# A two-layer Hyena / Mamba-2 / mixture-of-experts step: earlier modulation pieces, waits moved across stage seams, and the router in batches

## The reference

```python
sh1, sc1, g1, sh2, sc2, g2 = split(silu(cond) @ ada_w + ada_b, 6)   # once for the context, once for the latents
h = rmsnorm(x, g) * (1 + sc1) + sh1
u = dwconv(h @ in_w + in_b, short_w, short_b)                       # 3072 channels, 3 taps: x0, x1, v
f = sin(freq * (z @ w1 + b1)); f = sin(freq * (f @ w2 + b2))        # filter net, width 64
h_fwd, h_bwd = (f @ w3) * window
v = fft_long_conv(v * x1, h_fwd, h_bwd) + (v * x1) * bias
x = x + g1 * ((v * x0) @ out_w)
h2 = rmsnorm(x, g) * (1 + sc2) + sh2
aff = softmax(h2 @ w_router)                                        # 16 experts
gate, idx = top_k(aff.T, cap)                                       # 128 latent and 16 context rows an expert
x = x + g2 * scatter_add(gate * experts(h2[idx]))
```

## Time and profile before

| | us |
|---|---|
| median of three runs | 3776.02 |
| the profiled execution, its own time | 3775.25 |
| its span | 3773.3 |
| TensorE busy | 3405.7 (90%) |
| VectorE busy | 1868.8 (50%) |
| ScalarE busy | 1297.2 (34%) |
| GpSimd busy | 369.8 (10%) |

### The profile page before, as it was taken

How to read it: one execution, slowest core, us unless ns; L and a number is a source line. 1 busy time by engine, 2 the same in 40 slices (tenths; PEclk the granted TensorE clock), 3 DMA queues, 4 the chain that set the end, 5 groups by cost and what they waited for, 6 DMA issues and landing times. The chain is left out here.

```text
span 3773.3 us, 58905 instructions
## 1 busy us (share of the span) xinstructions
PE 3405.7 (90%) x24069; PEld 2934.9 (78%) x24069; DVE 1868.8 (50%) x3059; ACT 1297.2 (34%) x2067; POOL 369.8 (10%) x361
## 2 busy tenths in 40 slices
PE   4999888979499999998799999779996599999996
PEld 2999764748399999997699999746664499999995
DVE  6233286855533333333544554689996533333333
ACT  4232332224133333333532233266664133333332
POOL 0000000000011111111000000000000011111111
PEclk7999898989699999999799999989997799999998
DMA  6566323054588888885334443397776488888885
GB/s 233 165 207 207 108 83 148 33 195 168 190 289 289 289 289 289 289 288 171 86 106 131 148 142 105 126 341 245 257 255 230 154 290 289 289 289 289 289 289 193
DMA packets 413304, 799.49 MB, mean 212 GB/s; under 512 B 22135, under 2 KB 107836, under 8 KB 411851
## 3 DMA queue, kind: packets, MB, share of 16 engines
q1 hardware_dynamic: 383724, 699.32, 52.8%
q0 software_dynamic: 29232, 98.14, 8.8%
q10 hardware_dynamic: 208, 0.10, 0.0%
HBM read 688.59 MB, written 108.90 MB: 211 GB/s over the span
## 5 line engine op out<-in xcount | busy, mean ns | idle before, releaser
L2192 PEld LDWEIGHTS moe_banks<-moe_xt,mix_ring 128*128 128x128 f32 x8192 | 1012.6, 191 | 5.5 <-issue 3.2
L2192 PE MATMUL moe_banks<-moe_xt,mix_ring 128*128 128x144 f32 x8192 | 1013.9, 287 | 3.1 <-ACT moe_xt L2227 3.1
L62 PE MATMUL ssdin_banks<-h_leading,ssdin_w_split 128*128 128x384 f32 x1920 | 412.0, 344 | 0.0
L2272 DVE TENSOR_TENSOR moe_hid<-moe_banks,moe_sg 128x128 f32<-128x128 f32 x256 | 74.6, 291 | 582.2 <-ACT moe_sg L2250 582.2
L2214 PE MATMUL moe_banks<-moe_down_parts,moe_hid_parts 128*128 128x512 f32 x1536 | 357.5, 392 | 0.0
L62 PEld LDWEIGHTS ssdin_banks<-h_leading,ssdin_w_split 128*128 128x128 f32 x1920 | 337.2, 188 | 14.4 <-issue 13.6
L2214 PEld LDWEIGHTS moe_banks<-moe_down_parts,moe_hid_parts 128*128 128x128 f32 x1536 | 285.9, 188 | 71.3 <-issue 13.2
L2262 DVE TENSOR_TENSOR moe_down_parts<-mix_ring,moe_down_parts 128x2048 fp32r<-128x2048 f32 x128 | 292.2, 2283 | 0.0
L3151 PE MATMUL scan_banks<-scan_w,scan_yc 128*128 128x512 f32 x576 | 254.8, 596 | 0.0
L62 PE MATMUL hyin_banks<-h_leading,hyin_w_split 128*128 128x384 f32 x1152 | 238.0, 338 | 11.5 <-DVE hyin_w_split L751 11.5
L2159 POOL DMA_INDIRECT x_dram<-moe_yc,mix_idx_quarter x128 | 166.3, 1299 | 820.1 <-DVE moe_yc L2283 790.8
(11 more groups left out here) (442 smaller groups left out, 4448.5 us busy)
## 6 DMA issues: line engine op xcount, KB each, us to landing
mix_ring<-in_moe_w_gate SPq DMA_DIRECT2D x64, 2048.0 KB, 8.1
mix_ring<-in_moe_w_up SPq DMA_DIRECT2D x64, 2048.0 KB, 13.1
mix_ring<-in_moe_w_down SPq DMA_DIRECT2D x64, 2048.0 KB, 16.0
early_ring<-in_ada_w SPq DMA_DIRECT2D x96, 512.0 KB, 5.4
scan_cum<-row_dram SPq DMA_DIRECT2D x36, 1024.0 KB, 6.2
ssd_w<-in_ssd_in_w SPq DMA_DIRECT2D x40, 512.0 KB, 4.1
s_dram<-ssdin_work SPq DMA_DIRECT2D x64, 256.0 KB, 2.1
scan_states<-s_dram SPq DMA_DIRECT2D x32, 512.0 KB, 7.7
```

What stands on the lines that cost most here:

```text
L62: ins = pe.matmul(out(piece), w_at(w[a], k), h_k(h[b], k, piece), start=(k == 0 and a == 0 and b == 0), stop=(k == KD - 1 and a == 1))
L2192: ins = pe.matmul(pb[:, 2 * (f % 2) + j, 0:SLOTS], ring[:, 2 * half + j, k, col:col + P], xt[:, k, :], start=(k == 0), stop=(k == KD - 1))
L2272: dve.tensor_tensor(hid[:, f % 2, :], up[:, 0:CAP_LAT], sg[:, f % 2, 0:CAP_LAT], ALU.mult).then_inc(s_hid, 1)
```

## The change

In the opening TensorE multiplies piece 0 ahead of the parameter rows, piece 1 ahead of the filter's first layer, pieces 2 and 3 behind it in the two banks of pieces 0 and 1, and the filter's second layer after all pieces. VectorE's list follows, with the first position add ahead of the gain columns. The second angles and the second sine move into the projection (angles ahead of VectorE's first tile, sine behind ScalarE's second; TensorE waits for the angles before its second tile). `front_h` gets three buffers. The first two weight splits of the projection move into the last rounds of the opening's tile loop. To make that possible, the opening and the projection share one set of banks, and the filter's buffers lie under those of the split rows.

At the seams: the last x0 and u stores of the projection are issued by SyncE and waited for in the convolution, by SyncE before it loads u and by ScalarE before its first filter copy; the g stores are waited for in the output projection, before its first load; the last two x stores of the scan are waited for in the second router, before the loads of those tiles. In the convolution one ScalarE copy (the context row, L1186) moves ahead of `keep_filter(5)`.

VectorE subtracts the trailing part of the same two splits in the same round. `HF` is 3. The class `Router` gets the scheme of `phase_route`: partial logits, a summing matmul, the logits kept, softmax in batches of five and four tiles. In both routers the exponential, the quotients and the transposes of the first batch move into the loop.

```diff
@@ phase_front
-        hf = m.sb("h", [P, 2, KD, P])
+        hf = m.sb("h", [P, HF, KD, P])
-        PIECE_BANK = (3, 4, 5, 6)
+        PIECE_BANK = (3, 4, 3, 4)
@@ tensor
+                pe.wait_ge(s_silu, 2)
+                mod.product(pe, 0, pb[:, PIECE_BANK[0], 0:P])
                 pe.wait_ge(s_stage, 16 * (len(keep["param_rows"]) + 6))
...
-                pe.wait_ge(s_silu, 2)
+                mod.product(pe, 1, pb[:, PIECE_BANK[1], 0:P])
                 filt.products(pe, pb, 0)
-                mod.product(pe, 0, pb[:, PIECE_BANK[0], 0:P])
-                mod.product(pe, 1, pb[:, PIECE_BANK[1], 0:P])
-                filt.products(pe, pb, 1)
-                mod.product(pe, 2, pb[:, PIECE_BANK[2], 0:P])
-                mod.product(pe, 3, pb[:, PIECE_BANK[3], 0:P])
+                for n in range(2, FRONT_PIECES):
+                    pe.wait_ge(s_row, n - 1)
+                    mod.product(pe, n, pb[:, PIECE_BANK[n], 0:P])
                 pe.wait_ge(s_row, FRONT_PIECES)
...
+                filt.products(pe, pb, 1)
@@ phase_front, scalar
+                    if t == TILES:
+                        for q in range(2):
+                            act.wait_ge(keep["s_hy_w"][q], 16)
+                            act.activation(split[:, q, 0, :, :], w[:, q, :, :], ACT.Copy).then_inc(s_wh, 1)
@@ phase_hyena_in
+                sp.wait_ge(s_cv, HY_TILES)
+                store_x0(sp, LAST_BLOCK, keep["s_last_stored"])
+                sp.wait_ge(s_ur, HY_TILES)
+                store_u(sp, LAST_BLOCK, keep["s_last_stored"])
...
+                    if q == 1:
+                        filt.sine(act, 1)
...
+                filt.angles(dve, pb, 1)
@@ phase_long_conv
-                    keep_filter(5)
                     act.wait_ge(s_u, h * 16 + 16)
                     act.activation(win_r[:, 0, :], ut[:, 0, :], ACT.Copy).then_inc(s_zh, 1)
+                    keep_filter(5)
                     keep_filter(6)
...
-                sp.wait_ge(s_gs, 16 * 2 * CT_HALF)
@@ class Router
+    def partial_logits(self, pe, t):
...
+        for k in range(KD):
+            j = k % 4
+            ins = pe.matmul(self.part[self.COLS * j:self.COLS * (j + 1), :], self.wr[:, k, :], self.ht[:, k, :],
+                            start=(k < 4), stop=(k >= 4))
...
     def logits(self, pe, t):
...
-        for k in range(KD):
-            ins = pe.matmul(self.logit, self.ht[:, k, :], self.wr[:, k, :], start=(k == 0), stop=(k == KD - 1))
+        pe.matmul(self.logit, self.parts[:, :], self.adder[:, :], start=True, stop=True).then_inc(self.s_lg, 1)
@@ phase_hyena_out
+                sp.wait_ge(keep["s_g_stored"], 16 * KD)
                 load_g(0)
...
                     if t < TILES:
                         project(t, 0)
-                    if 2 <= t <= TILES + 1:
-                        router.logits(pe, t - 2)
-                    if t >= 3:
-                        router.turn_affinities(pe, t - 3)
+                    if t >= 2:
+                        router.partial_logits(pe, t - 2)
                     if t < TILES:
                         project(t, 1)
+                    if t >= 2 and t <= TILES:
+                        router.logits(pe, t - 2)
                     if 1 <= t <= TILES:
                         router.turn(pe, t - 1)
+                    if t == TILES:
+                        router.turn_affinities(pe, 0)
+                router.logits(pe, TILES - 1)
+                router.turn_affinities(pe, 1)
@@ phase_route
+                    if t >= TILES - 2:
+                        sp.wait_ge(keep["s_scan_x_stored"][t % 2], 16 * (t // 2 + 1))
                     load_x(t)
@@ phase_scan
-                for b in range(2):
-                    sp.wait_ge(s_st[b], 16 * (5 - b))
```

More of the change, by code:

```diff
@@ L174, in phase_front @@
         stage = m.sb("stage", [P, 4, P])
-        filt = Filter(m, io, keep["filt"], keep["prm"])
+        filt = keep["filter_net"]
+        filt.weights(m)
+        HF = 3
+        w, split = keep["hy_w"], keep["hy_split"]
+        s_wh, s_wl = keep["s_hy_lead"], keep["s_hy_rest"]
         d_all = m.sb("d_all", [P, 1, HEADS])
@@ L383, in _ @@
                 dve.wait_ge(s_done, 4)
+                piece(1)
                 filt.angles(dve, pb, 0)
+                piece(2)
+                piece(3)
                 dve.wait_ge(s_d, 16)
@@ L410, in _ @@
                         tile_evict(t - 1)
+                    if t == TILES:
+                        for q in range(2):
+                            dve.wait_ge(s_wh, q + 1)
+                            dve.tensor_tensor(split[:, q, 1, :, :], w[:, q, :, :], split[:, q, 0, :, :].bitcast(F32),
+                                              ALU.subtract).then_inc(s_wl, 1)
 def modulation_columns(dve, keep, layer, c, ks, shift, scale, s_gain):
@@ L569, in phase_hyena_in @@
         w = keep["hy_w"]
-        split = m.sb("w_split", [P, 2, 2, KD, P], F32R)
+        split = keep["hy_split"]
+        filt = keep["filter_net"]
         pad = m.sb("pad", [P, 2, GAPPED + 2])
@@ L838, with __init__ @@
     WIDTH = FOLD // PIECES
-    def __init__(self, m, io, filt, prm):
-        self.io, self.filt = io, filt
+    BANK = (0, 5)
+    def __init__(self, nc, m, io, filt, prm, columns, later):
+        self.io, self.filt, self.col = io, filt, columns
         self.bias, self.freq = [prm[:, 3, F_ROW + n:F_ROW + n + 1] for n in range(2)], prm[:, 3, F_ROW + 2:F_ROW + 3]
-        self.z = m.sb("tap_clock", [HY_EMB, TAPS])
-        self.w1 = m.sb("f_w1", [HY_EMB, HY_HID])
-        self.w2 = m.sb("f_w2", [P, HY_HID])
-        self.col = m.sb("f_columns", [P, 2])
-        self.arg = m.sb("angle", [P, FOLD])
-        self.turns = m.sb("turns", [P, FOLD])
-        self.h1 = self.turns
+        with ExitStack() as until_lead:
+            self.z, arg, turns = [until_lead.enter_context(nc.sbuf_tensor("filter_" + name, shape, F32)) for name, shape in
+                                  (("clock", [HY_EMB, TAPS]), ("angle", [P, FOLD]), ("turns", [P, FOLD]))]
+        self.arg, self.turns = (arg, later[:, 0:FOLD]), (turns, later[:, FOLD:2 * FOLD])
+        self.h1 = turns
         self.s_in = m.sem("filter_in")
@@ L875, in products @@
                     w, src = self.w1[:, :], self.z[:, half * FOLD + cols:half * FOLD + cols + self.WIDTH]
-                ins = pe.matmul(pb[at, n, 0:self.WIDTH], w, src, start=True, stop=True)
+                ins = pe.matmul(pb[at, self.BANK[layer] + n, 0:self.WIDTH], w, src, start=True, stop=True)
         ins.then_inc(self.s_mm, 1)
@@ L1617, in _ @@
                 lead(1)
-                for t in range(TILES + 3):
-                    if 2 <= t <= TILES + 1:
-                        router.exps(act, t - 2)
+                for t in range(TILES + 2):
+                    if t >= 2:
+                        router.keep_parts(act, t - 2)
                     if 1 <= t <= TILES:
@@ L1627, in _ @@
                         lead(t + 2)
+                    if t == TILES - 1:
+                        router.exps(act, 0)
+                router.exps(act, 1)
             @block.gpsimd
@@ L1709, in _ @@
                 position(1)
-                for t in range(TILES + 3):
-                    if 2 <= t <= TILES + 1:
-                        router.top(dve, t - 2)
-                    if t >= 3:
-                        router.keep_affinities(dve, t - 3)
-                    if 2 <= t <= TILES + 1:
-                        router.soft(dve, ch, t - 2)
+                for t in range(TILES + 2):
                     if t < TILES:
@@ L1722, in _ @@
                     position(t + 2)
+                    if t == 7:
+                        router.shift(dve, ch, 0)
+                    if t == TILES:
+                        router.soft(dve, ch, 0)
+                        router.keep_affinities(dve, 0)
+                        router.keep_affinities(dve, 1)
+                router.shift(dve, ch, 1)
+                router.soft(dve, ch, 1)
+                router.keep_affinities(dve, 2)
 PIECES = 6
@@ L3049, in phase_scan @@
         s_x = [m.sem(f"x_in{b}") for b in range(2)]
-        s_st = [m.sem(f"x_stored{b}") for b in range(2)]
+        s_st = keep["s_scan_x_stored"]
         s_one = m.sem("ones_ready")
@@ L3406, in build @@
             "s_const": ctx.enter_context(nc.semaphore("const_in")),
+            "s_scan_x_stored": [m.sem(f"scan_x_stored{b}") for b in range(2)],
         }
```

225 lines of the change are left out of this document (142 added, 83 removed).

## The result

The changed kernel took 3735.34 us (median of four runs, 3734.21 to 3739.16), beside 3776.14 for the kernel before on the same chip. The ratio is 0.9893, with a 95% interval of 0.9876 to 0.9910: 34 to 47 us off. In a later series the same kernel took 3736.89 us beside 3775.35, ratio 0.9904 (0.9888 to 0.9919). The ratios are the recorded estimates over all runs; they can differ by up to 0.0006 from the quotient of two medians. I forecast 3745, with a range of 3738 to 3754.

What follows compares the result with a forecast made beforehand. TensorE, busy 90% of a 3773.3 us span, bounds the kernel, mostly in matmul stretches the change doesn't touch. Terms of 8.0, 1.7, 5.4, 6.4, 1.3, 5.7 and 2.3 sum to 30.8 us off: 3745 us, range 3738 to 3754.

Steps and rivals of the forecast that it cites:

- Convolution: Inside each convolution half: moving the context row's copy ahead removes TensorE's 3.23 us wait, 6.4 us off, bounds 4 and 6.6.
- Third buffer and splits: Tile loop and first projection weights: ScalarE's eviction waits go, splits move into last rounds; 1.7 us off, bounds 0.5 and 3.
- Opening: Kernel start: multiplying modulation pieces as their slots land removes idle of the DMA engines; 8.0 us off, bounds 5 to 11.
- loss of 3.0: Opening: first filter layer between products 1 and 2, at most four slots in flight, costs 3.0 us of new fetch idle.
- gain of 2.3: Opening: the second filter layer leaves the fetch, whose rate had dropped from 31 to 37 us; counted at 2.3 us.
- Seams: Stage ends no longer wait for store landings: convolution 5.4, output projection 1.3, second router 2.3 us off.
- Output projection: Router in the output projection: partial logits and a sum matmul save 0.81 us in seven tiles, 5.7 us; bounds 4 and 7.5.
- tails: Ends of the output projection and second router after the last tile: no change, 0 plus or minus 0.5 us each.
- rival (d): Output projection router: draining costs 1 us at each change of form, 12 us more, 3757 us; chance 0.04.
- Projection: The big projection's body keeps its code, order and operands; costed at nothing, 0 us.
- Rivals (a) to (d): Opening keeps half its gap, 0.13; convolution's wait handed on, 0.08; seam waits pass to readers, 0.09; form changes drain TensorE, 0.04.
- Rival (e): Projection: TensorE stays at 1.2 GHz; gain gone from 62 us on, 3785 us after 80 us; chance 0.02.

## Why the prediction was right in its places and short in its sum

**Convolution (forecast 6.4, measured 10.1): the step that failed.** The mechanism was right and so was what came next, TensorE itself. The term was mis-sized: I took the idle time as the price of the wait, and set the upper bound at 6.6 by the same reading. The other half stood in the earlier trace rows: 16 products take 5.53 us behind the wait, and 8 of the same form beside it 1.98. These 3.7 us are some two fifths of the miss, and alone they would have brought the forecast to 3741.

**Third buffer and splits (1.7, measured 3.5).** I counted 2.4 us for the third buffer, all at the loop's end, and nothing in the middle, where VectorE is full. That step failed too, by 0.2 us a round: the buffer is worth 4.0 to 4.4, and the measured 3.5 lies outside my bound of 3. Moving the splits costs 0.5 us; my sum had 0.7 for it (2.36 + 0.6 in the loop, 2.3 back behind it).

**Opening (8.0, measured 7.5).** The size is right, by luck, and the parts are not: the order alone gives it all. The hole behind the first filter layer is there (1.9 us of idle, by the shares from 27 to 30 us), but closing it gained nothing, so the loss of 3.0 doesn't show in the time; nor does the gain of 2.3 from the second layer.

**Seams (5.4, 1.3 and 2.3; measured 5.8, 2.1 and 2.3).** Right in size. That the landings are saved and not handed on holds in all three: 3.7, 2.1 and 2.3 us come back when they are waited for. The middle one was short by 0.8, inside its bound of 2.3: the load behind it also became faster, which I had not counted.

**Output projection (5.7, measured 5.9) and tails (0, measured 0.4 and 0.5).** The router's body was right to 0.04 us a tile, and rival (d) is out. I walked the second router's tail through and found 0; it gains 1.27 at the upper clock, which my bound of 0.5 didn't allow, and 0.5 over all profiles.

**Projection (0, measured -0.9).** Not foreseen; no row of before could have shown it.

**The range.** Nearly all errors had one sign, and my bounds, taken as independent, let them average out. The bound that was plainly too tight is the convolution's (6.6 against 10.1). Rivals (a) to (d) all lay above the forecast, and none asked what a wait costs beside its own length; the range had no case on the side where the time fell. Rival (e), the low clock lasting, did not come: the first piece's product comes 14.8 us after the projection's first matmul, 15.1 before.

## What to carry to other kernels

A wait of TensorE can cost more than its idle time, here 5.07 us for 3.23: compare the first matmuls behind it with the same form elsewhere in the profile, and count the difference too. Where a wait can't be removed, products that nobody reads can hold the clock, if they last until the next real work. And where a full engine alternates two buffers, look for an instruction that waits for its own engine's last one: a third buffer can gain on an engine that never shows idle time.

## What the hardware showed that I had not expected

- At the convolution's wait the granted clock fell after the idle time, not in it: it was still 0.96 in the two microseconds that hold most of the wait, and 0.50 only in the window after the one in which TensorE had begun again. Behind the idle products ahead of the projection it fell inside the gap, some 2.7 us into 4.16.
- A gap of 2.23 us left the next products at 1.13 us for four, the full clock's time, and one of 3.23 us did not.
- Slots of 512 KB released one by one kept the DMA engines from ever being idle and yet moved 238 GB/s, where the same fetch with a hole in it moved 257 and 266.
- Two allocations of the same buffer made the same 1,728 matmuls of the projection 0.8 to 1.1 us slower in sum; between the pieces' products most groups of three tiles take 14.63, 14.80 and 15.40 us with the slower placing, 14.65, 14.59 and 15.42 with the old one.
